# A mixture-of-experts stage in a one-core Trainium2 kernel: shift and scale of the routed rows moved from the experts' loop into the routing stage, onto GpSimd

## The chip, the cores and the metric

The kernel runs on one core of a Trainium2 chip. The metric is the device time of one execution in microseconds (us), as the median of several runs. The core has TensorE (PE, with its weight loads listed as PEld), VectorE (DVE), ScalarE (ACT), GpSimd (POOL) and SyncE (SP); SP computes nothing and issues most DMAs.

## The reference, cut to what matters

The reference is two transformer blocks in float32 (512 latent tokens and 256 context tokens of width 1024). The first block ends in a hierarchical mixture of experts, which is what the change is about:

```python
h = modulate(rms_norm(x, norm_ffn_g), shift, scale)      # h * (1 + scale) + shift
def hier_moe(h, w_rg, b_rg, w_re, b_re, w_gate, w_up, w_down):
    g_logits = hf @ w_rg + b_rg                          # 4 groups, the best one is taken
    e_logits = hf @ w_re + b_re                          # 32 experts, top 2 inside the group
    ...
    # rows of a token go to blocks of one expert, padded
    yb = (silu(xi @ w_gate[e]) * (xi @ w_up[e])) @ w_down[e]
    y = segment_sum(yb * row_w, row_tok)
```

`shift` and `scale` are two vectors of 1024 (one for all latent tokens), computed early from the conditioning vector; the gain `norm_ffn_g` is a third. The rms norm is a factor for each token; the modulation is a factor and a summand for each of the 1024 columns.

## The kernel before, in words

The program is one long sequence of stages. At the end of a stage every engine runs `fence` (line 222): it drains, counts up the semaphore `stage_done`, and the four compute engines wait for each other. SP isn't in the fence; its loads wait for semaphores and for given values of `stage_done`.

The last product ahead of the mixture (`pe_out`, `dve_resid`) ends at about 579 us; then fence 9 falls. In the **norm and routing stage** `act_norm` (line 447) sums squares, `dve_norm` (line 470) writes the four tiles of 128 tokens, scaled by their rms factor, to `XK(t)` (line 479), TensorE turns them (line 427), and ScalarE and VectorE shift and scale each turned quarter on its way out of PSUM into `hT` (lines 456 and 487), from which TensorE computes the router's logits (line 1557). SP stores `XK(t)`, only normed, to `xnd` in HBM as each tile is ready (line 3254). Then `dve_route` (line 1592) works out groups, experts, slots and weights in some seventy small operations on VectorE with a drain between most of them, with TensorE for prefix sums and for the list of token rows. The 128x1024 comparison `LOW` (line 1700) comes near its end. The last operation releases `rows_ok`; GpSimd, which has nothing else to do in this stage, waits for it and for the four stores, and gathers the first 128 rows from `xnd` (line 1725). Fence 10 falls.

Three small vectors, shift, scale and gain, come by three loads of 8 elements a partition at the start (`sp_route_params`, line 1541), and VectorE forms gain x (1 + scale) from them in column layout (line 1615).

The **experts' loop** (`sp_moe`, `pool_moe`, `pe_moe`, `act_moe`, `dve_moe`, lines 1741 to 1823) has 16 rounds here, each of two experts with 64 rows. Round i, in order: TensorE turns the 128x1024 gathered rows into PSUM banks 0 and 1 (line 1766). ScalarE takes bank 0 in four quarters and VectorE bank 1 in four quarters into `xgT`, and both shift and scale each quarter with one number a partition (lines 1797 and 1815). TensorE multiplies with the gate weights and the up weights (line 1775), ScalarE applies Silu (line 1801), VectorE multiplies (line 1820), TensorE turns the product (line 1780), ScalarE copies it out (line 1803), TensorE multiplies with the down weights (line 1788), VectorE applies the output gate vector (line 1823) and ScalarE's queue stores 128x1024 rows (line 1805). VectorE enters the loop only when the gate vector, loaded by ScalarE's queue after fence 10 (line 1396), is there. GpSimd gathers the next round's rows (line 1755) as soon as TensorE has turned the present ones. SP loads the six matrices of the next round (2 MB each, line 1739), the two of each kind as soon as their buffer has been used. The matrices of the first round are loaded during the stages before: up and down from 552 us, gate after fence 9.

Of the kernel before, what the change touches and what calls it, by code (L numbers as in the profile page):

```python
# [23 lines left out]
ALU = mybir.AluOpType  # L24
ACT = mybir.ActivationFunctionType
# [84 lines left out]
def program(nc, I, out):  # L110
    ctx = ExitStack()
    with ctx:
# [11 lines left out]
        def sem(name):  # L124
            return ctx.enter_context(nc.semaphore(name))
# [23 lines left out]
        def bank(b, n=BANK):  # L149
            return ps[:, b * BANK:b * BANK + n]  # L150
# [52 lines left out]
        v2a, a2v, v2p, prm = sem("v2a"), sem("a2v"), sem("v2p"), sem("prm")  # L203
        out_in, gate_in = sem("out_in"), sem("gate_in")
        rparams, zero_ok, rows_ok = sem("rparams"), sem("zero_ok"), sem("rows_ok")
        xg_in, xn_st = sem("xg_in"), sem("xn_st")
        w_used = [sem(f"w_used{m}") for m in range(3)]
        w_in_ = [sem(f"w_in{m}") for m in range(6)]
# [13 lines left out]
        def fence(eng, n):  # L222

            eng.drain().then_inc(stage_done, 1)  # L224
            n["fence"] += 4
            eng.wait_ge(stage_done, n["fence"])
# [319 lines left out]
        def plan_lin1(n):  # L546
            return Plan(n, "av" * 16 + "av")
# [131 lines left out]
        def plan_norm1(n):  # L679
            return Plan(n, "-" * (2 * TA))  # L680
# [717 lines left out]
        def plan_turn3(n, nt):  # L1398
            p = Plan(n, "v" * (2 * nt))
            p.g0 = n.get("t3", 0)  # L1400
            n["t3"] = p.g0 + 2 * nt
            return p
# [125 lines left out]
        EID = Z[0:1, 7780:7828].bitcast(I32)  # L1528
        NIT = Z[0:1, 7828:7829].bitcast(I32)
        SLOT, HS, LO8 = Z[:, 7640:7648], Z[:, 7648:7656], Z[:, 7656:7664]  # L1530
        TKB, IOTA, S8 = Z[:, 8800:8928], Z[:, 9824:9952], Z[:, 7664:7672]
        GE = Z[:, 5600:5800].rearrange("p (a j) -> p a j", j=25)
        HIT = Z[:, 5984:6176].rearrange("p (a j) -> p a j", j=24)
        LOW = Z[:, 8800:9824].rearrange("p (a j) -> p a j", j=P)
# [1 line left out]
        def sp_route_params(sp):  # L1536
            sp.dma_start(rw[:, :, 0:NG], I["router_group_w"][0].rearrange("(k p) n -> p k n", p=P)).then_inc(rparams, 16)
            sp.dma_start(rw[:, :, NG:NG + NE], I["router_expert_w"][0].rearrange("(k p) n -> p k n", p=P)).then_inc(rparams, 16)
            sp.dma_start(rb[:, 0:NG], I["router_group_b"][0].partition_broadcast(P)).then_inc(rparams, 16)
            sp.dma_start(rb[:, NG:NG + NE], I["router_expert_b"][0].partition_broadcast(P)).then_inc(rparams, 16)  # L1540
            for dst, src in ((fsh, modd[0, 0, 3 * D:4 * D]), (fsc, modd[0, 0, 4 * D:5 * D]), (fga, I["norm_ffn_g"][0])):
                sp.dma_start(dst, src.rearrange("(p k) -> p k", k=KT)).then_inc(rparams, 16)

        fsh, fsc, fga, fA = (small[:, 1240 + 8 * i:1248 + 8 * i] for i in range(4))

        def plan_route(n):
            return Plan(n, "vvvvv")
# [1 line left out]
        def pe_logits(pe):  # L1549

            def each(p, t):
                if t == 0:
                    pe.wait_ge(rparams, 16 * 7)
                for i in (2 * t, 2 * t + 1):
                    pe.wait_ge(EV[p.own[i]], p.val[i])
                for k in range(KT):
                    last = nc.tensor.matmul(bank(4)[:, 36 * t:36 * t + 36], hTk[:, k, 128 * t:128 * t + 128], rw[:, k, :],
                                            start=(k == 0), stop=(k == KT - 1))
                if t == TL - 1:
                    last.then_inc(mm_done, 1)  # L1560
            return each
# [30 lines left out]
        def dve_route(dve, n):  # L1592
# [18 lines left out]
                D_()  # L1611

            V.tensor_copy(TKB, C(C_TK, 1).broadcast_to([P, P])).then_inc(v2p, 1)
            dve.wait_ge(rparams, 16 * 7)
            V.scalar_tensor_tensor(fA, fsc, 1.0, fga, ALU.add, ALU.mult)
            dve.wait_ge(mm_done, p.done(0))
            V.tensor_tensor(LG, bank(4)[:, 0:36 * TL].rearrange("p (t n) -> p t n", t=TL), rb.unsqueeze(1).broadcast_to([P, TL, 36]),
                            ALU.add).then_inc(evac_v, 1)
# [77 lines left out]
            for c in range(2):  # L1696
                h = HIT[:, TL * c:TL * c + TL, :]
                V.tensor_tensor(h, h, C(C_TK, TL).unsqueeze(2).broadcast_to([P, TL, 24]), ALU.mult)
            D_()
            V.tensor_tensor(LOW, wide(LO8, P), IOTA.unsqueeze(1).broadcast_to([P, 2 * TL, P]), ALU.is_equal).then_inc(v2p, 1)  # L1700
            for c in range(2):
                V.tensor_copy(IDX[:, c, :], sc(10 + c))
# [18 lines left out]
        def pool_route(pool):  # L1721

            pool.wait_ge(rows_ok, 1)
            pool.wait_ge(xn_st, 16 * TL)
            pool.indirect_dma_start(xg, None, xnd, bass.IndirectOffsetOnAxis(ap=ROWS[:, 0:1].bitcast(U32), axis=0)).then_inc(xg_in, 16)
# [66 lines left out]
        def act_moe(act):  # L1792
            nit = trips(act)
            with act.Fori(0, nit) as i:
                act.wait_ge(xt_done, 2 * i + 3)
                for k in range(4):
                    last = act.activation(xgT[:, k, :], bank(0)[:, 128 * k:128 * k + 128], ACT.Identity,  # L1797
                                          scale=fA[:, k:k + 1], bias=fsh[:, k:k + 1])
                last.then_inc(xt_a, 1)
                act.wait_ge(w_used[0], i + 2)  # L1800
                act.activation(hg, bank(2), ACT.Silu).then_inc(silu_ok, 1)
                act.wait_ge(ht_done, i + 1)
                act.activation(hd, bank(4), ACT.Copy).then_inc(ht_a, 1)
                act.wait_ge(y_v, i + 1)
                act.dma_start(ybuf[bass.ds(i * P, P), :], yo).then_inc(y_out, 16)
            act.wait_ge(y_out, 16 * nit + 16)
            act.sem_inc(y_stored, 1)

        def dve_moe(dve, n):
            n["gate"] += 32  # L1810
            dve.wait_ge(gate_in, n["gate"])
            with dve.Fori(0, trips(dve)) as i:
                dve.wait_ge(xt_done, 2 * i + 4)
                for k in range(4):
                    last = nc.vector.tensor_scalar(xgT[:, 4 + k, :], bank(1)[:, 128 * k:128 * k + 128], fA[:, 4 + k:5 + k],
                                                   fsh[:, 4 + k:5 + k], ALU.mult, ALU.add)
                last.then_inc(xt_v, 1)
                dve.wait_ge(silu_ok, i + 1)
                dve.wait_ge(w_used[1], i + 2)
                nc.vector.tensor_tensor(hu, hg, bank(3), ALU.mult).then_inc(hu_ok, 1)  # L1820
                dve.wait_ge(w_used[2], i + 2)
                dve.wait_ge(y_out, 16 * i + 16)
                nc.vector.tensor_tensor(yo, ps[:, 5 * BANK:7 * BANK], gtb[:, 0, :], ALU.mult).then_inc(y_v, 1)
# [1406 lines left out]
        @block.sync  # L3230
        def _(sp):
            n, rel = tally(), [0, 0]
            sp_first(sp)
            plan_norm1(n)
            sp_lin1(sp, n, rel)
            sp.wait_ge(stage_done, 4 * 3)
            sp.dma_start(xl[:, 0:TL, :], I["x"][0].rearrange("(t p) d -> p t d", p=P)).then_inc(x_again, 16)
            for plan in (plan_gate, plan_dec, plan_st, plan_o):
                plan(n)
            plan_turn3(n, TL)  # L3240
            sp_out(sp, n, rel, I["w_out"][0], WO1, 0)
            sp.wait_ge(stage_done, 4 * 8)
            sp_route_params(sp)
            sp.dma_start(xl[:, TL:TA, :], I["ctx_2"][0].rearrange("(t p) d -> p t d", p=P)).then_inc(x_in, 16)
            for m in (1, 2):
                for x in range(2):
                    load_expert(sp, m, x, slice(x, x + 1))
            sp.wait_ge(stage_done, 4 * 9)
            for x in range(2):
                load_expert(sp, 0, x, slice(x, x + 1))  # L3250

            for t in range(TL):
                sp.wait_ge(xn_ok, TA + t + 1)
                sp.dma_start(xnd[P * t:P * t + P, :], XK(t)).then_inc(xn_st, 16)
            plan_norm(n, TL)
            plan_route(n)
            sp.wait_ge(stage_done, 4 * 10)
            sp_moe(sp)
            n["fence"] = 4 * 12
            plan_attn(n, *da_spec())  # L3260
            sp.wait_ge(stage_done, 4 * 12)
            for l in range(2):
                sp_layer(sp, n, rel, l)
            for t in LAT:
                sp.wait_ge(fin_ok, t + 1)
                sp.dma_start(out[0, P * t:P * t + P, :], yacc[:, t, :]).then_inc(out_in, 16)
            sp.wait_ge(stage_done, 4 * NF)
            sp.wait_ge(out_in, 64)

        @block.gpsimd  # L3270
        def _(pool):
# [23 lines left out]
            pool_glao(pool)  # L3295
            for _ in range(3):
                fence(pool, n)
            pool_route(pool)
            fence(pool, n)
            pool.dma_start(fng, I["final_norm_g"].partition_broadcast(P)).then_inc(fng_in, 16)  # L3300
# [1 line left out]
            fence(pool, n)  # L3302
            pool_comb(pool)
            fence(pool, n)
            plan_norm1(n)
            plan_lin1(n)
            for plan in (plan_gate, plan_dec, plan_st, plan_o):
                plan(n)
            plan_turn3(n, TL)
            plan_lin(n, WO1)  # L3310
            plan_norm(n, TL)
            plan_route(n)
            plan_attn(n, *da_spec())
            for l in range(2):
# [138 lines left out]
```

## Time and profile before

| | us |
|---|---|
| median of 3 runs | 3842.81 (3840.83 to 3851.01) |
| the profiled execution | 3844.6, its span 3842.7 |
| PE busy | 3374.2 (88%) |
| DVE busy | 1623.2 (42%) |
| ACT busy | 1132.2 (29%) |
| POOL busy | 617.5 (16%) |
| norm and routing stage | 579 to 627 |
| experts' loop | 639 to 1137 |

The busy times are sums over the whole span, with stages of different limits; what a change in one stage is worth has to be read in that stage. Times in the rows below are microseconds from the start of the span. The difference between a profiled execution's time and its span lies outside the span.

### The profile page before, as it was taken

The numbers are of one execution on the slowest core, as the hardware profiler recorded it, in microseconds if no ns is written. First come the engines' busy times: TensorE is split into PE (matmuls) and PEld (weight loads), VectorE is DVE, ScalarE is ACT, GpSimd is POOL, SyncE is SP. The second block draws the span as 40 slices with busy tenths as digits, with TensorE's granted clock in tenths as the row PEclk, the third lists the DMA queues.
The fourth block names the chain that finished last, engine by engine and source line by source line (L and its number), as shares of the span: only waits on it lengthen the run. The fifth ranks groups of instructions, "written<-read, shape, count | busy, mean of one in ns | idle before, by whom it ended". The sixth has DMA issues, their size and how long they took to land. (4 is left out here: it accounts for less than half of the span.)

```text
span 3842.7 us, 41657 instructions
## 1 busy us (share of the span) xinstructions
PE 3374.2 (88%) x16325; PEld 2395.6 (62%) x16325; DVE 1623.2 (42%) x2697; ACT 1132.2 (29%) x1921; POOL 617.5 (16%) x452
## 2 busy tenths in 40 slices
PE   4999875887766989789999799999799899988999
PEld 2666663222225865447887688888685457867887
DVE  3335653000015635563433533334574564345445
ACT  3113522111113235443222321221234444323222
POOL 1000000000003334123220100000345123301000
PEclk8999887899987999999999899999899999999999
DMA  6884034999986210002112312112521003224232
GB/s 255 327 323 164 3 123 190 428 428 428 428 353 204 62 25 11 9 36 84 57 55 88 112 65 66 60 62 88 161 73 35 9 36 107 84 107 138 88 99 88
DMA packets 162107, 534.00 MB, mean 139 GB/s; under 512 B 11917, under 2 KB 67077, under 8 KB 138893
## 3 DMA queue, kind: packets, MB, share of 16 engines
q1 hardware_dynamic: 139196, 401.22, 28.0%
q0 software_dynamic: 16256, 92.05, 6.8%
q10 hardware_dynamic: 6480, 38.34, 2.5%
q8 instruction: 117, 1.92, 0.2%
q14 instruction: 58, 0.47, 0.0%
HBM read 488.82 MB, written 42.76 MB: 138 GB/s over the span
## 5 line engine op out<-in xcount | busy, mean ns | idle before, releaser
L2981 PE MATMUL ps<-hT_hi,w_hi 128*128 128x512 f32 (+1 forms) x768 | 275.7, 359 | 24.6 <-DVE w_lo L2022 24.6
L2981 PE MATMUL ps<-hT_hi,w_lo 128*128 128x512 f32 (+1 forms) x768 | 276.3, 360 | 0.0
L2981 PE MATMUL ps<-hT_lo,w_hi 128*128 128x512 f32 (+1 forms) x768 | 275.9, 359 | 0.0
L2987 PE MATMUL ps<-w_hi,h_hi 128*128 128x512 f32 x640 | 253.7, 396 | 0.0
L2987 PE MATMUL ps<-w_hi,h_lo 128*128 128x512 f32 x640 | 253.7, 396 | 0.0
L2987 PE MATMUL ps<-w_lo,h_hi 128*128 128x512 f32 x640 | 253.6, 396 | 0.0
L2026 PE MATMUL ps<-wp_hi,hT_hi 128*128 128x512 f32 (+2 forms) x608 | 222.2, 365 | 30.6 <-DVE wp_lo L2022 29.1
L2243 PE MATMUL ps<-Z 64*128 64x256 f32 (+3 forms) x576 | 200.2, 544 | 29.1 <-DVE small L2385 12.2
L2027 PE MATMUL ps<-wp_lo,hT_hi 128*128 128x512 f32 (+2 forms) x608 | 220.2, 362 | 0.0
L2028 PE MATMUL ps<-wp_hi,hm_lo 128*128 128x512 f32 (+2 forms) x608 | 220.2, 362 | 0.0
L3004 ACT ACTIVATE w_hi<-ring 128x2048 fp32r<-128x2048 f32 x62 | 118.3, 1908 | 326.8 <-PE ps L2987 326.8
L2683 POOL TENSOR_TENSOR mr_lo<-ring,wm_hi 128x2048 fp32r<-128x2048 f32 x34 | 160.4, 4722 | 302.8 <-ACT wm_hi L2675 302.4
L1775 PE MATMUL ps<-ring,Z 128*64 128x512 f32 x512 | 144.2, 727 | 64.0 <-ACT Z L1797 59.9
L2026 PE MATMUL ps<-wm_hi,hT_hi 128*128 128x512 f32 x480 | 191.0, 398 | 8.8 <-ACT hT_hi L2739 8.8
L2027 PE MATMUL ps<-mr_lo,hT_hi 128*128 128x512 f32 x480 | 191.6, 399 | 0.0
L2027 PE MATMUL ps<-w_lo,hT_hi 128*128 128x512 f32 x480 | 191.2, 398 | 0.0
L2028 PE MATMUL ps<-wm_hi,hm_lo 128*128 128x512 f32 x480 | 191.1, 398 | 0.0
L2981 PEld LDWEIGHTS ps<-hT_hi,w_hi 128*128 128x128 f32 x768 | 145.0, 189 | 48.8 <-issue 25.0
L3038 DVE TENSOR_TENSOR w_lo<-ring,w_hi 128x2048 fp32r<-128x2048 f32 x62 | 142.1, 2292 | 76.4 <-ACT w_hi L3004 76.4
L3061 DVE TENSOR_TENSOR pj<-pj,ps 128x512 f32<-128x512 f32 x140 | 95.6, 686 | 167.4 <-PE ps L2987 167.4
L2981 PEld LDWEIGHTS ps<-hT_lo,w_hi 128*128 128x128 f32 x768 | 145.2, 189 | 24.6
L2981 PEld LDWEIGHTS ps<-hT_hi,w_lo 128*128 128x128 f32 x768 | 145.8, 190 | 23.0
(474 smaller groups left out, 6687.3 us busy)
## 6 DMA issues: line engine op xcount, KB each, us to landing
pj<-in_expert_w_up_dram SPq DMA_DIRECT2D x32, 2048.0 KB, 23.7
pj<-in_expert_w_down_dram SPq DMA_DIRECT2D x32, 2048.0 KB, 19.7
ring<-in_expert_w_gate_dram SPq DMA_DIRECT2D x32, 2048.0 KB, 15.5
ring<-in_ffn_w_dram SPq DMA_DIRECT2D x64, 1024.0 KB, 5.2
ring<-in_w_in_dram SPq DMA_DIRECT2D x58, 1024.0 KB, 5.4
Z<-in_w_mod_dram POOLq DMA_DIRECT2D x24, 2048.0 KB, 8.1
Z<-in_w_ada_dram POOLq DMA_DIRECT2D x8, 2048.0 KB, 8.7
ring<-in_w_out_dram SPq DMA_DIRECT2D x12, 1024.0 KB, 10.3
```

The costliest lines, as they stand in the source:

```text
L1775: last = nc.tensor.matmul(bank(2 + m)[64 * x:64 * x + 64, :], xgT[:, k, 64 * x:64 * x + 64], mslot[2 * m + x][:, 512 * k:512 * k + 512], s ...
L2026: nc.tensor.matmul(out_, a_hi, b_hi, start=first, stop=False)
L2027: nc.tensor.matmul(out_, a_hi, b_lo, start=False, stop=False)
L2028: return nc.tensor.matmul(out_, a_lo, b_hi, start=False, stop=final)
L2243: return nc.tensor.matmul(A.lat(u, x) if k0 == 0 else A.ctx(u, x), S["kq"](p, x, "q")[rs, P * t:P * t + P], S["kq"](p, x, "k")[rs, P * k0: ...
L2683: pool.tensor_tensor(mr_lo[:, 2048 * (x % 4):2048 * (x % 4) + 2048], mring[x % 4], wm_hi[:, 2048 * (x % 3):2048 * (x % 3) + 2048], ALU.sub ...
L2981: last = nc.tensor.matmul(bank(i % 8, c1 - c0), W[a][:, k, :], r[:, k, c0:c1], start=(k == 0 and r is hhk and a == 0), stop=(k == KT - 1 a ...
L2987: last = nc.tensor.matmul(bank(i % 8), H1[hb % 2][a][:, k, P * what:P * what + P], W[b][:, k, :], start=(k == 0 and a == b), stop=(k == 3 ...
L3004: act.activation(WHI[x % 2], raw[x % 4], ACT.Copy).then_inc(w_hi_ok, 1)
L3038: nc.vector.tensor_tensor(WLO[x % 2], raw[x % 4], WHI[x % 2], ALU.subtract).then_inc(w_lo_ok, 1)
L3061: nc.vector.tensor_tensor(y, y, bank(i % 8), ALU.add).then_inc(out_read, 1)
```

## The change

The rows that are stored to `xnd` are now normed, scaled and shifted, so that in the loop both engines only copy the turned rows. SP loads the three vectors as full rows, the same on all 128 partitions (512 KB each), after fence 9 and ahead of the gate weights. GpSimd forms (1 + scale) x gain, and then for each tile, once TensorE has turned it, multiplies and adds in place. SP stores a tile when GpSimd's sum for it is done. `RG` shares its place with `LOW`, so VectorE waits for GpSimd's first product before `LOW`.

```diff
+        mrow_in, mrow_ok, xm_ok = sem("mod_rows_in"), sem("mod_rows_ok"), sem("xm_ok")
...
-        TKB, IOTA, S8 = Z[:, 8800:8928], Z[:, 9824:9952], Z[:, 7664:7672]
+        RSH, RSC, RG = pj[:, 17408:18432], pj[:, 16384:17408], Z[:, 8800:9824]
+        TKB, IOTA, S8 = Z[:, 9952:10080], Z[:, 9824:9952], Z[:, 7664:7672]
...
-            for dst, src in ((fsh, modd[0, 0, 3 * D:4 * D]), (fsc, modd[0, 0, 4 * D:5 * D]), (fga, I["norm_ffn_g"][0])):
-                sp.dma_start(dst, src.rearrange("(p k) -> p k", k=KT)).then_inc(rparams, 16)
-
-        fsh, fsc, fga, fA = (small[:, 1240 + 8 * i:1248 + 8 * i] for i in range(4))
+
+        def sp_mod_rows(sp):
+            for dst, src in ((RSC, modd[0, 0, 4 * D:5 * D]), (RG, I["norm_ffn_g"][0]), (RSH, modd[0, 0, 3 * D:4 * D])):
+                sp.dma_start(dst, src.partition_broadcast(P)).then_inc(mrow_in, 16)
+
+        def pool_mod_rows(pool, p):
+
+            pool.wait_ge(mrow_in, 16 * 3)
+            pool.tensor_scalar(RSC, RSC, 1.0, 1.0, ALU.add, ALU.mult)
+            pool.drain()
+            pool.tensor_tensor(RSC, RSC, RG, ALU.mult)
+            pool.drain().then_inc(mrow_ok, 1)
+            for t in range(TL):
+                pool.wait_ge(mm_done, p.done(2 * t + 1))
+                pool.tensor_tensor(XK(t), XK(t), RSC, ALU.mult)
+                pool.drain()
+                pool.tensor_tensor(XK(t), XK(t), RSH, ALU.add).then_inc(xm_ok, 1)
...
-                    pe.wait_ge(rparams, 16 * 7)
+                    pe.wait_ge(rparams, 16 * 4)
...
-            dve.wait_ge(rparams, 16 * 7)
-            V.scalar_tensor_tensor(fA, fsc, 1.0, fga, ALU.add, ALU.mult)
+            dve.wait_ge(rparams, 16 * 4)
...
             D_()
+            dve.wait_ge(mrow_ok, 1)
             V.tensor_tensor(LOW, wide(LO8, P), IOTA.unsqueeze(1).broadcast_to([P, 2 * TL, P]), ALU.is_equal).then_inc(v2p, 1)
...
-                for k in range(4):
-                    last = act.activation(xgT[:, k, :], bank(0)[:, 128 * k:128 * k + 128], ACT.Identity,
-                                          scale=fA[:, k:k + 1], bias=fsh[:, k:k + 1])
-                last.then_inc(xt_a, 1)
+                act.activation(xgT[:, 0:4, :], bank(0).rearrange("p (k n) -> p k n", k=4), ACT.Copy).then_inc(xt_a, 1)
...
-                for k in range(4):
-                    last = nc.vector.tensor_scalar(xgT[:, 4 + k, :], bank(1)[:, 128 * k:128 * k + 128], fA[:, 4 + k:5 + k],
-                                                   fsh[:, 4 + k:5 + k], ALU.mult, ALU.add)
-                last.then_inc(xt_v, 1)
+                nc.vector.tensor_copy(xgT[:, 4:8, :], bank(1).rearrange("p (k n) -> p k n", k=4)).then_inc(xt_v, 1)
...
             sp.wait_ge(stage_done, 4 * 9)
+            sp_mod_rows(sp)
             for x in range(2):
                 load_expert(sp, 0, x, slice(x, x + 1))
 
             for t in range(TL):
-                sp.wait_ge(xn_ok, TA + t + 1)
+                sp.wait_ge(xm_ok, t + 1)
                 sp.dma_start(xnd[P * t:P * t + P, :], XK(t)).then_inc(xn_st, 16)
...
+            pool_mod_rows(pool, plan_norm(n, TL))
             pool_route(pool)
```

(On GpSimd the counting calls `plan_norm1`, `plan_lin1` and so on, which issue no instruction, move ahead of this call, so that it knows the counts of `mm_done`.)

## Rows read from the trace of the kernel before

**Rows 1.** Windows: busy us (count) of each engine, PE clock, DMA share, GB/s.

```profile
600.00:610.00 10.00, 3.12 (x15) 3.13 (x15) 5.85 (x28) 0.42 (x2) 0.00 (x0) 0.50 0.00 1
...
700.00:760.00 60.00, 50.52 (x216) 17.44 (x216) 6.37 (x12) 9.08 (x15) 1.75 (x4) 0.90 1.01 428
```

**Rows 2.** Timeline of one round of the loop: start, us, engine, line, operation [idle before].

```profile
882.43 1.22 DVE L1823 TENSOR_TENSOR Z<-ps,Z 128x1024 f32<-128x1024 f32 x1 [9.20 <-PE ps L1788]
...
884.51 1.28 ACT L1797 ACT_TABLE_LOAD   x1 [9.85 <-DVE Z L1823]
...
885.81 1.51 ACT L1797 ACTIVATE Z<-ps,small 128x128 f32<-128x128 f32 x4
...
887.37 8.41 PE L1775 MATMUL ps<-ring,Z 128*64 128x512 f32 x32 [3.98 <-ACT Z L1797]
...
897.27 7.09 PE L1775 MATMUL ps<-pj,Z 128*64 128x512 f32 x32 [1.49 <-DMA pj<-in_expert_w_up_dram]
...
905.92 0.60 ACT L1803 ACTIVATE Z<-ps 128x512 f32<-128x512 f32 x1 [9.49 <-PE ps L1780]
```

**Rows 3.** Groups of VectorE by form: busy us, mean ns, idle before.

```profile
L3059 DVE COPY pj<-ps 128x512 f32<-128x512 f32 x20 | 13.7, 690 | 26.5 <-PE ps L2987 26.5
```

**Rows 4.** Timeline at the start of the loop.

```profile
626.67 1.06 POOL L1725 DMA_INDIRECT Z<-xnd,Z  x1 [132.63 <-DVEq L224]
...
637.79 1.37 DVE L1815 TENSOR_SCALAR Z<-ps,small 128x128 f32<-128x128 f32 x4 [12.01 <-issue]
...
639.26 9.58 PE L1775 MATMUL ps<-ring,Z 128*64 128x512 f32 x32 [4.18 <-issue]
```

**Rows 5.** Timeline of the last round, and the window in which its weights end.

```profile
1111.98 8.75 PE L1775 MATMUL ps<-ring,Z 128*64 128x512 f32 x32 [3.98 <-ACT Z L1797]
...
1129.82 7.09 PE L1788 MATMUL ps<-pj,Z 128*64 128x512 f32 x32 [0.69 <-ACT Z L1803]
...
1127.00:1128.00 1.00, 0.59 (x4) 0.00 (x0) 0.35 (x1) 0.00 (x0) 0.00 (x0) 1.00 0.28 115
```

**Rows 6.** Timeline of the norm and routing stage.

```profile
579.42 0.80 SPq L1739 DMA_DIRECT2D ring<-in_expert_w_gate_dram  x2
...
589.47 0.74 DVE L479 TENSOR_SCALAR Z<-xl,small 128x1024 f32<-128x1024 f32 x1
...
601.38 0.49 DVE L1635 TENSOR_TENSOR Z<-Z 128x32 f32<-128x32 f32 x4
```

**Rows 7.** The same timeline: the gate vector's loads, 512 KB each.

```profile
631.55 0.81 ACTq L1396 DMA_DIRECT2D Z<-modd  x2
```

**Rows 8.** Groups of GpSimd by form: busy us, mean ns, idle before.

```profile
L2895 POOL TENSOR_SCALAR pj<-xl,small 128x1024 f32<-128x1024 f32 x11 | 16.0, 1471 | 227.0 <-DVE small L2864 227.0
...
L1307 POOL TENSOR_TENSOR pj<-pj,Z 128x512 f32<-128x512 f32 x4 | 4.9, 1264 | 157.1 <-DVEq L224 157.1
```

**Rows 9.** Timelines of VectorE and GpSimd in later stages where both run.

```profile
1237.47 4.47 DVE L1040 TENSOR_TENSOR Z<-pj 128x512 f32<-128x512 f32 x1
1242.01 0.69 DVE L1042 TENSOR_REDUCE small<-Z 128x8 f32<-128x512 f32 x1
1242.62 1.50 DVE L1040 TENSOR_TENSOR Z<-pj 128x512 f32<-128x512 f32 x1
...
1236.77 4.62 POOL L1985 TENSOR_TENSOR wp_lo<-ring,wp_hi 128x2048 fp32r<-128x2048 f32 x1 [3.24 <-ACT wp_hi L1971]
1241.35 2.22 POOL L1914 TENSOR_TENSOR Z<-Z,consts 128x896 f32<-128x896 f32 x1
...
2853.12 3.96 DVE L1044 TENSOR_SCALAR small<-small 128x4 f32<-128x4 f32 x1
...
2863.42 4.62 DVE L1040 TENSOR_TENSOR Z<-pj 128x128 f32<-128x128 f32 x1
...
2852.22 4.83 POOL L1985 TENSOR_TENSOR wp_lo<-ring,wp_hi 128x2048 fp32r<-128x2048 f32 x1 [11.39 <-ACT wp_hi L1971]
2863.26 4.63 POOL L1985 TENSOR_TENSOR wp_lo<-ring,wp_hi 128x2048 fp32r<-128x2048 f32 x1 [6.21 <-ACT wp_hi L1971]
```

More of the change, by code:

```diff
@@ L3297, in _ @@
                 fence(pool, n)
+            plan_norm1(n)
+            plan_lin1(n)
+            for plan in (plan_gate, plan_dec, plan_st, plan_o):
+                plan(n)
+            plan_turn3(n, TL)
+            plan_lin(n, WO1)
+            pool_mod_rows(pool, plan_norm(n, TL))
             pool_route(pool)
@@ L3304, in _ @@
             fence(pool, n)
[L3305 to L3311, printed above, removed]
             plan_route(n)
```

## The prediction

> **What bounds the kernel now.** The change touches two neighbouring stages, so I first read the windows by stage. They show two different limits. In the routing stage (about 597 to 627 us) VectorE works through a serial chain of small operations; between 600 and 610 us it is busy 5.85 of 10 us, GpSimd is busy 0, and the DMA engines are empty. In the experts' loop (639 to 1137 us, 16 rounds of 31.8 us) the DMA share is 1.01 at 428 GB/s in each of six windows of 60 us from 700 to 1060, of which the first is shown [rows 1]. A round moves six matrices of 2048 KB, one gather of 512 KB and one store of 512 KB, 13.6 MB: at 428 GB/s that is 31.8 us, exactly the round. The loop is bound by the weights' transfer.
>
> Next I read the timeline of one round [rows 2]. After the down product the queue in front of the gate product is: VectorE's scaling of the result (ends at 883.65), then on ScalarE (whose queue issues the store first) a table load of 1.28 us, four activations of 1.50 us together, then TensorE's gate product at 887.37. So ScalarE's turn costs 2.9 us that TensorE waits for. But the up product then waits 1.49 us for its own weights: what TensorE gains ahead of the gate product it returns there.
>
> **What goes in the loop.** ScalarE's four activations become one Copy of 128x512; the row for the same form (hd from a PSUM bank) is 0.60 us and is preceded by no table load [rows 2]. Gain in front of the gate product: 1.28 + 1.51 - 0.60 = 2.2 us a round. VectorE's four operations of 1.37 us together become one copy of 128x512 from PSUM, 0.69 [rows 3]: 0.7 us. If the Silu still gets a table load in each round, it lies under the gate product of over 8 us and costs nothing.
> - In rounds 1 to 14 I count nothing: the stream of weights covers it. Without that cover it would be 15 x 2.2 = 33 us.
> - In the first round the gate product waits for VectorE, which waits for the gate vector until 637.79 and ends at 639.16; TensorE starts at 639.26 [rows 4]. With one copy it starts 0.7 us sooner, and so does the first weight load of the loop and with it the whole stream: -0.7.
> - In the last round the stream has ended by 1127.3 [rows 5], while the down product starts only at 1129.82 and waits for ScalarE and so for the chain gate product, up product, turn. The gate product of that round starts at 1111.98; 2.2 sooner moves the down product to 1127.6, still just behind the last weights. So -2.2.
>
> About ScalarE's table: the rows show a load in front of the first Identity in each of the rounds, and none in front of the Copy. The Trainium skill, "ScalarE: Activation LUTs", section "Table sets: the hidden batching unit", says that cheap functions, copy and identity among them, are in every set. By that rule the load ahead of Identity would not be there and the exchange would give only 0.9 in place of 2.2; this trace does not bear it out.
>
> **What comes into the routing stage.** SP issues three row loads of 512 KB (128 x 4 KB) right after stage 9 closes at 579.42, in front of the two gate loads [rows 6]. The DMA engines are then idle. The nearest row is the gate vector: two such loads issued at 631.55 let VectorE go at 637.79, 6.2 us, with a third one beside them [rows 4, 7]. I take 7 us for three: 586.5. Ends: 585 (two loads' 6 us less the third beside them) and 590 (the 4 MB of gate weights behind them take part of the engines). The gate weights themselves land some 4 us later and are first used at 639: nothing. SP's three small loads that go away free its queue 2.5 us sooner for weights that nobody waits for: nothing. VectorE loses one small operation, 0.2.
>
> GpSimd then does one tensor-scalar of 128x1024, 1.5 us [rows 8], one product, and per tile a product and a sum: nine tensor-tensor of 128x1024. No row has that form. The row of 512 elements gives 1.26 us (2.47 ns an element), that of 2048 gives 4.62 (2.26) [rows 8, 9]; bounds 2.1 and 2.5, I take 2.3, nearest to the line between them, and 0.25 for the drain and the hand-over. 586.5 + 1.6 + 9 x 2.55 = 611 us is its end. The last tile's store is issued then and, at no more than the 6.2 us of the gate vector, is there by 617. The gather waits for the slots (626.67 before [rows 4]), so the stores are covered by 9 us and more. The new wait of VectorE ahead of the 128x1024 comparison (behind it are the last routing product and the gather) is fulfilled near 591, 29 us ahead: nothing.
>
> **What it does to VectorE** is the term that decides. The timelines of both engines show it against GpSimd's tensor-tensor [rows 9]: a 128x512 tensor-tensor of 0.68 lasts 4.47 us, until GpSimd's of 4.62 us has ended; the tensor-reduce behind it passes in 0.69; the next tensor-tensor takes 1.50, again until GpSimd's second has ended; and that second one took 2.22. Small ones are not spared: 128x128 lasts 4.62, a tensor-scalar of 128x4 3.96. So while GpSimd runs one tensor-tensor after another, VectorE gets about one operation that reads two SBUF tensors, or one in its fast form, through for each of them; reduces and operations on PSUM pass.
>
> Stepping VectorE's order through nine slots of 2.55 us from 588.1: the scalings of tiles 2 and 3 (589.47 before) take slots 1 and 2, the copy of the token column slot 4, the 16-element comparisons, product and subtraction of the first choice slots 5 to 8, the tensor-scalar after the exponential slot 9. At 611.3 VectorE stands where it stood at 601.38 [rows 6]. Each slot passes one operation which takes 0.3 us otherwise, so how many there are hardly matters: the delay is GpSimd's end less 601.3, and is **10 us**. Bounds: 585 with 2.1 a product gives 606.5 and 5 us; 590 with 2.5 gives 617 and 16 us; 0 if nothing is held. All behind it (slots, gather, fence, the gate vector's load, the first round) moves along, since nothing there waits for anything else: the engines are idle or in this chain.
>
> **The sum.** +10 - 0.7 - 2.2 = +7.1 us on the profiled execution's 3844.6 (span 3842.7, rest outside it unchanged): 3851.7. The median of the three runs lies 1.8 below that execution, so 3850. A measurement of this kernel can tell about 0.3%, 11.5 us, from no change.
>
> **The rivals.**
> - *VectorE is not held* (20%): the small operations slip in between GpSimd's, or GpSimd waits instead. For: no row has a chain of drained small operations. Against: [rows 9]. Then only the gain stays, -2.9: 3840; with a part of the holds up to 3845. The Trainium skill, "SBUF — State Buffer", section "Who interferes with whom", says that the loser blocks fully for the whole instruction; by that this rival would fall.
> - *The rows come late, GpSimd is slow* (16%), the other side: the three row loads share the engines with the gate weights and land at 590 or later, and each product is 2.5 plus 0.35 of waiting for VectorE's operation in between. GpSimd ends at 590 + 1.6 + 9 x 2.85 = 617.3, the delay is 16, the sum +13: 3856. It decides from a delay of 14.4 us on, which is a GpSimd end behind 615.7.
> - *The loop is not bound by its transfer* (3%): 2.2 us in each round, 33 us, less the delay of 10: 3820. Against it: DMA share 1.01, and 13.6 MB at 428 GB/s is the round.
> - *The exchange saves nothing in the loop* (the table load stays ahead of the Copy; 6%): then +10 - 0.7 - 0.9 = +8.4, 3851, hardly to be told apart from the forecast.
>
> **How the numbers follow.** The forecast has 55%. Same (within 0.3%) holds the forecast, the first and the last rival: 0.80; slower 0.17, faster 0.03. The range reaches from the first rival with its 1 us less, 3839, to the late case, 3858.
>
> **What would show it.** Right: VectorE's small operations in the routing stage with durations near 2 us, one for each GpSimd product; the first gather issued near 636 instead of 626.67; rounds still 31.8 us, with the gate product starting 2.2 us sooner behind the down product and the up product waiting 3 to 4 us for its weights. Wrong: the gather at 627 (nothing held), or behind 641 (the late case, or the stores ending the wait); rounds of under 31.5 us; a table load still in front of ScalarE's Copy.

## The result, and the profile after

The kernel after takes 3854.14 us, the kernel before 3846.76 (medians of 20 runs each); the ratio is 1.002 with a 95% interval of 1.0014 to 1.0026. The change costs 7.4 us by the medians, where +7.1 was forecast. (The 3842.81 of the table above is the median of the first three of the runs before.) The profiled execution of after took 3849.9 us, its span 3848.0, 5.3 over the span before.

Two executions differ by some microseconds in stages that no line of the change touches, so I count from points inside the trace: from the first sum of squares behind fence 9 (579.42 before, 577.30 after) to VectorE's last operation of the routing stage, to the issue of the first gather, and from there to the last result's scaling behind the loop.

| us | before | after |
|---|---|---|
| fence 9 to VectorE's last operation | 46.18 | 54.80 |
| fence 9 to the first gather | 47.25 | 55.31 |
| first gather to the last result's scaling | 510.38 | 508.15 |

The span's +5.3 is then: -2.1 ahead of fence 9 (another execution), +8.1 in the routing stage, -2.2 in the loop, +1.6 behind it (again another execution; nothing there was changed).

The timeline of VectorE after, from the end of the norms into the first choice; it answers to [rows 6]:

```profile
587.35 1.24 DVE L480 TENSOR_SCALAR Z<-xl,small 128x1024 f32<-128x1024 f32 x1
588.51 1.36 DVE L488 TENSOR_SCALAR hT<-ps,small 128x128 f32<-128x128 f32 x4
589.79 1.56 DVE L480 TENSOR_SCALAR Z<-xl,small 128x1024 f32<-128x1024 f32 x1
...
594.37 1.59 DVE L1629 COPY Z<-consts 128x128 f32<-128x128 f32 x1
...
597.49 0.91 DVE L1620 TENSOR_TENSOR Z<-Z 128x16 f32<-128x16 f32 x1
598.48 2.22 DVE L1622 TENSOR_TENSOR Z<-Z,consts 128x16 f32<-128x16 f32 x1
600.77 0.17 DVE L1624 TENSOR_REDUCE Z<-Z 128x4 f32<-128x16 f32 x1
601.01 2.17 DVE L1626 TENSOR_TENSOR Z<-Z 128x16 f32<-128x16 f32 x1
603.25 2.22 DVE L1640 TENSOR_TENSOR Z<-Z 128x16 f32<-128x16 f32 x1
...
606.10 1.86 DVE L1646 TENSOR_SCALAR Z<-Z 128x16 f32<-128x16 f32 x1
607.87 0.48 DVE L1650 TENSOR_TENSOR Z<-Z 128x32 f32<-128x32 f32 x4
```

And that of GpSimd in the same stretch, with the gather behind it:

```profile
584.49 1.04 POOL L1551 TENSOR_SCALAR pj<-pj 128x1024 f32<-128x1024 f32 x1 [91.66 <-DMA pj<-modd]
585.69 2.36 POOL L1553 TENSOR_TENSOR pj<-pj,Z 128x1024 f32<-128x1024 f32 x1 [0.15 <-issue]
588.22 2.59 POOL L1557 TENSOR_TENSOR Z<-Z,pj 128x1024 f32<-128x1024 f32 x1 [0.18 <-issue]
...
603.11 2.34 POOL L1557 TENSOR_TENSOR Z<-Z,pj 128x1024 f32<-128x1024 f32 x1
605.59 2.34 POOL L1559 TENSOR_TENSOR Z<-Z,pj 128x1024 f32<-128x1024 f32 x1
632.61 1.08 POOL L1741 DMA_INDIRECT Z<-xnd,Z  x1 [24.69 <-DVEq L1735]
```

The two are to be read side by side. Operations on 16 elements last 2.2 us: the one that starts at 598.48 ends at 600.7, where GpSimd's instruction of 598.33 (2.34 us) ends; the tensor-reduce behind it takes 0.17 and isn't held; the next one lasts until 603.18, again to the end of GpSimd's next instruction. The four quarters from PSUM (588.51) keep their 1.36. From 607.93, when GpSimd is done, every duration is as before. Line 1650 is line 1635 of before: it stood at 601.38 - 579.42 = 21.96 us behind the fence, and now at 30.57.

The loop. The timeline of one round after answers to [rows 2]:

```profile
889.75 0.34 ACTq L1818 DMA_DIRECT2D ybuf<-Z  x1
890.44 1.28 ACT L1812 ACT_TABLE_LOAD   x1 [9.37 <-DVE Z L1833]
...
891.74 0.60 ACT L1812 ACTIVATE Z<-ps 128x512 f32<-128x512 f32 x1
892.35 1.28 ACT L1814 ACT_TABLE_LOAD   x1
892.39 7.09 PE L1791 MATMUL ps<-ring,Z 128*64 128x512 f32 x32 [3.08 <-ACT Z L1812]
...
901.97 7.09 PE L1791 MATMUL ps<-pj,Z 128*64 128x512 f32 x32 [2.49 <-DMA pj<-in_expert_w_up_dram]
```

The Copy takes 0.60 in place of 1.51 us, but the table load in front of it stays: TensorE waits 3.08 us ahead of the gate product where it waited 3.98. The windows and the waits of the loop after:

```profile
700.00:760.00 60.00, 45.47 (x211) 17.52 (x212) 3.43 (x5) 8.33 (x10) 1.79 (x3) 1.00 1.01 428
...
1000.00:1060.00 60.00, 48.64 (x206) 17.94 (x202) 5.02 (x6) 8.71 (x10) 2.30 (x4) 0.91 1.01 428
...
PE ps L1791 <- ACT Z L1812: 46.2, 15, 3.1
PE ps L1791 <- DMA pj<-in_expert_w_up_dram: 31.9, 13, 3.7
```

In the waits of before the same two were:

```profile
PE ps L1775 <- ACT Z L1797: 59.9, 15, 4.0
...
PE ps L1775 <- DMA pj<-in_expert_w_up_dram: 8.0, 7, 1.5
```

TensorE waits 13.7 us less for ScalarE and 23.9 us more for the up weights, at the same 428 GB/s as in [rows 1]. The second figure is larger because several gate products are shorter too (7.09 us at 892.39 in place of 8.4 to 9.5 us before), and it scatters: in e1, e2, e3, e8 and e10 below, which have the same loop, TensorE waits 9.5 to 33.1 us for the up weights beside the same 46 us for ScalarE. The 15 rounds between the first and the last gate product take 472.7 us before and 471.0 after.

### The profile page after: what moved, and what is told of

The parts are those of the page before. It is cut to its first block and busy times, and to the rows that moved or that the text cites. A ratio compares the mean times of both kernels' runs of the same rounds, so it can differ in the third digit from the quotient of the medians.

```text
span 3848.0 us, 41576 instructions
## 1 busy us (share of the span) xinstructions
PE 3362.2 (87%) x16325; PEld 2392.5 (62%) x16325; DVE 1623.4 (42%) x2648; ACT 1117.7 (29%) x1873; POOL 641.5 (17%) x462
## 5 line engine op out<-in xcount | busy, mean ns | idle before, releaser
L2253 PE MATMUL ps<-Z 64*128 64x256 f32 (+3 forms) x576 | 201.6, 544 | 28.7 <-DVE small L2395 12.6
L1791 PE MATMUL ps<-ring,Z 128*64 128x512 f32 x512 | 125.5, 647 | 49.9 <-ACT Z L1812 46.2
```

Source lines behind the costliest of these rows:

```text
L1791: last = nc.tensor.matmul(bank(2 + m)[64 * x:64 * x + 64, :], xgT[:, k, 64 * x:64 * x + 64], mslot[2 * m + x][:, 512 * k:512 * k + 512], s ...
L2253: return nc.tensor.matmul(A.lat(u, x) if k0 == 0 else A.ctx(u, x), S["kq"](p, x, "q")[rs, P * t:P * t + P], S["kq"](p, x, "k")[rs, P * k0: ...
```

## The experiments

Theory: GpSimd's nine reading instructions hold VectorE in the routing stage, and the transfer of the weights hides what the loop gains. Rivals: the late stores, the row loads or the denser stage cost the time; the loop's exchange has another value than it seems. The last columns of this table are read as above; ratios are to the kernel before.

| kernel | fence 9 to VectorE's last operation | first gather to last scaling | ratio, 95% |
|---|---|---|---|
| before | 46.18 | 510.38 | |
| after | 54.80 | 508.15 | 1.002 (1.0014 to 1.0026) |
| e1, GpSimd only writes | 46.39 | 509.62 | 0.9995 (0.9986 to 1.0004) |
| e2, products alone | 46.89 | 509.25 | 0.9994 (0.9984 to 1.0003) |
| e3, before with copying loop | 46.19 | 509.36 | 0.9996 (0.9987 to 1.0005) |
| e4, after with old loop | 54.84 | 509.37 | 1.002 (1.001 to 1.0029) |
| e8, turned back, late | 50.37 | 508.98 | 1.0007 (0.9998 to 1.0017) |
| e9, the same, turned loop | 50.35 | 510.47 | 1.0015 (1.0006 to 1.0024) |
| e10, turned back, in order | 46.27 | 510.93 | 0.9996 (0.9988 to 1.0005) |
| e11, the same, turned loop | 46.26 | 510.29 | 1.0006 (0.9997 to 1.0015) |

**e1: GpSimd as busy, but only writing.**

```diff
+            def busy():
+                for _ in range(2):
+                    last = pool.memset(pj[:, 16384:17604], 0.0)
+                    pool.drain()
+                return last
...
-            pool.tensor_tensor(RSC, RSC, RG, ALU.mult)
+            busy()
...
-                pool.tensor_tensor(XK(t), XK(t), RSC, ALU.mult)
-                pool.drain()
-                pool.tensor_tensor(XK(t), XK(t), RSH, ALU.add).then_inc(xm_ok, 1)
+                busy()
+                busy().then_inc(xm_ok, 1)
```

> The kernel after, but each of GpSimd's nine products and sums of the routing stage is replaced by two memsets of 1220 columns into the place of the row vectors, so GpSimd is busy for about as long (2.3 us each time) and only writes. Shift and scale of the experts' rows are left out. Routing time is counted from the first sum of squares after fence 9 to the issue of the first gather: 47.3 us before, 55.3 after. Theory (VectorE's operations that read two SBUF tensors, and its fast forms, are held while GpSimd's instruction reads): routing time falls to 47 to 48.5 us, the comparisons of the first choice take 0.17 to 0.3 us again, total near the kernel before, ratio 0.999 to 1.000. Rival (the late stores, the row loads or GpSimd's occupation itself delay the stage): it stays at 55 us, the stores being as late as after.

From GpSimd's and VectorE's timeline of this kernel:

```profile
590.88 20.29 POOL L1553 MEMSET pj<- 128x1220 f32 x16 [0.22 <-issue]
...
592.40 1.64 DVE L480 TENSOR_SCALAR Z<-xl,small 128x1024 f32<-128x1024 f32 x1
...
597.00 0.65 DVE L1633 COPY Z<-consts 128x128 f32<-128x128 f32 x1
...
600.13 0.18 DVE L1624 TENSOR_TENSOR Z<-Z 128x16 f32<-128x16 f32 x1
600.38 0.17 DVE L1626 TENSOR_TENSOR Z<-Z,consts 128x16 f32<-128x16 f32 x1
...
601.92 0.63 DVE L1650 TENSOR_SCALAR Z<-Z 128x16 f32<-128x16 f32 x1
```

GpSimd is busy to 611.2, 31.2 us behind the fence, as long as after, and the stores are as late. Yet VectorE's last operation comes at 46.39 us; the tensor-tensor operations that lasted 0.91 and 2.22 us take 0.18 and 0.17. All but 0.2 us of the delay of 8.6 us is gone, though row loads, late stores and the new wait are all still there. Some operations that read one SBUF tensor are still held beside the memsets: the scalings of tiles 2 and 3 take 1.23 and 1.64 us, as long as after, the copy of the token column 0.65 us in place of 0.21, and the tensor-scalar behind the exponential 0.63 in place of 0.14. The two-input operations of the chain are held only beside the reading instructions. Whether a GpSimd instruction that reads one tensor instead of two would hold them as well was not tested.

**e2: five reading instructions in place of nine.** The line with `ALU.add` is left out and its signal stands at the product.

> The kernel after without the four sums (the shift of the experts' rows is left out): five tensor-tensor on GpSimd in place of nine. Theory (one held operation for each GpSimd instruction, so the delay is GpSimd's end less the point VectorE had reached): GpSimd ends about 20.6 us behind fence 9, when the first choice's chain has hardly begun; routing time 48 to 49.5 us, a delay of 1 to 2. Rival (VectorE slowed in proportion to GpSimd's work): delay 5/9 of 8.1, so 51.7 us.

The timelines of GpSimd and VectorE of this kernel:

```profile
586.27 9.97 POOL L1557 TENSOR_TENSOR Z<-Z,pj 128x1024 f32<-128x1024 f32 x4 [0.18 <-issue]
...
595.51 0.75 DVE L1618 TENSOR_TENSOR Z<-Z 128x16 f32<-128x16 f32 x1
596.34 0.18 DVE L1620 TENSOR_TENSOR Z<-Z,consts 128x16 f32<-128x16 f32 x1
```

The delay is 0.7 us, not 5/9 of 8.6. GpSimd ends at 596.24, inside the first comparison of the choice; before that point VectorE reads mostly PSUM and few of its operations are held. So the four sums, with which GpSimd ends 9.7 us later behind the fence (30.6 in place of 20.9), cost 7.9 us of VectorE's time, and five products alone cost 0.7. (From the fence to the gather it was 47.41, under the 48 to 49.5 expected: the gather follows VectorE's last operation by 0.52 us in place of 1.07, see the last section, and the delay itself was under the 1 to 2 expected.)

**e3 and e4: the two halves of the change apart.** e3 is the kernel before with the loop of after:

```diff
-                for k in range(4):
-                    last = act.activation(xgT[:, k, :], bank(0)[:, 128 * k:128 * k + 128], ACT.Identity,
-                                          scale=fA[:, k:k + 1], bias=fsh[:, k:k + 1])
-                last.then_inc(xt_a, 1)
+                act.activation(xgT[:, 0:4, :], bank(0).rearrange("p (k n) -> p k n", k=4), ACT.Copy).then_inc(xt_a, 1)
```

and VectorE's alike; e4 is the kernel after with the reverse edit and the three column vectors loaded and formed as before.

> The kernel before with nothing changed but the loop: ScalarE and VectorE only copy the turned rows, so shift and scale of the experts' rows are left out. Theory (the loop is bound by the weights' transfer): routing time 47.3 us as before; from the first gather to the last result's scaling 508.2 us in place of 510.4, as in the kernel after; ratio 0.9994, not to be told from 1. Rival (the exchange pays in each round, 0.9 us by the rows of after): 496 us, ratio 0.996.

> The kernel after with the loop of before (four operations a bank with the column vectors, loaded and formed again), so shift and scale are applied twice. Theory: routing time 55.3 us as after, loop 510.4 us as before; total 2.2 us over the kernel after, ratio to before 1.002 to 1.003. If the loop's part of the change were larger than it seems, the loop would take over 512 us here.

e3 has the routing time of before, e4 that of after; the loss lies wholly in the routing stage. The loop shows no such order: 509.36 us with copies in e3, where 508.2 was expected, 509.37 with four operations in e4, where 510.4 was expected, and over all copying loops 508.2 to 510.9. What the exchange gives there is under this scatter of 2.8 us from profile to profile. The 2.2 us less in the one profile of after can't be put down to the exchange.

**e5, e6, e7: the loop without its cover.** In the rounds SP loads half of each matrix:

```diff
-                        load_expert(sp, m, x, bass.ds(e[x], 1))
+                        sp.dma_start(mslot[2 * m + x][:, 0:HALF // 2], WE[m][bass.ds(e[x], 1)].rearrange("a (p k) n -> p (a k n)", p=P)[:, 0:HALF // 2]).then_inc(w_in_[2 * m + x], 16)
```

e5 has the old loop, e6 the copying one, and e7 turns ScalarE's loop:

```diff
+            take(3)
+            with act.Fori(1, nit) as i:
+                act.wait_ge(w_used[0], i + 1)
+                act.activation(hg, bank(2), ACT.Silu).then_inc(silu_ok, 1)
+                act.wait_ge(ht_done, i)
+                act.activation(hd, bank(4), ACT.Copy).then_inc(ht_a, 1)
+                act.wait_ge(y_v, i)
+                act.dma_start(ybuf[bass.ds(i * P - P, P), :], yo).then_inc(y_out, 16)
+                take(2 * i + 3)
...
```

(`take` waits for the turned rows and issues the Copy; the last round's part stands behind the loop.)

> The kernel before, but in the loop SP loads only half of each expert's matrix (1 MB in place of 2 MB; the experts' weights are wrong from the second round on). A round then moves 7.3 MB, 17 us at 428 GB/s, so TensorE's chain must be the bound. Summed from the rows of the kernel after, with no wait for weights: 27.7 us a round with copies and 0.9 more with four operations a bank, so 28.6 us here. This one alone tells nothing between the theories; it is the base for the next.

> The same with the copying loop (shift and scale left out). Theory (the exchange is worth 0.9 us a round, which the transfer of the weights hides in the full kernel): 27.7 us a round, 0.9 less than with half loads and the old loop. Rival (the exchange is worth nothing on TensorE's chain in any case, since another wait takes its place): the same round.

> The same again, with ScalarE's loop turned: the first Copy stands ahead of the loop and each round begins with the Silu and ends with the next round's Copy. Theory (the table load in front of the Copy is there because the Copy is the first activation behind the loop's head): the load ahead of the Copy is gone, one load a round or none, at the Silu, hidden; 26.4 us a round, 1.3 less. Rival (each Copy behind a Silu costs a load): two loads a round still, 27.7 us.

TensorE's gate products in a round of e5, e6 and e7:

```profile
883.36 9.46 PE L1775 MATMUL ps<-ring,Z 128*64 128x512 f32 x32 [3.99 <-ACT Z L1797]
```

```profile
902.31 8.78 PE L1775 MATMUL ps<-ring,Z 128*64 128x512 f32 x32 [3.08 <-ACT Z L1796]
```

```profile
897.81 7.09 PE L1775 MATMUL ps<-ring,Z 128*64 128x512 f32 x32 [1.58 <-ACT Z L1797]
```

The rounds are 30.72, 29.01 (28.88 and 29.14 in turn) and 25.93 us, where 28.6, 27.7 and 26.4 were expected; the times of the one run of each are 3836.83, 3808.16 and 3764.12 us. So the exchange does pay where the weights come fast enough: 1.7 us a round, and turning the loop 3.1 more. Both are larger than the ScalarE time they save (0.9 and 1.5), since the gate product gets shorter as well, from 9.46 us to 8.53 and 8.79 in turn and then to 7.09. What makes it shorter is TensorE's granted clock. In e5 it falls to its lower level (0.50, which is 1.2 GHz) while TensorE idles ahead of the gate product, and stays there through its first half. From the windows of e5:

```profile
883.00:884.00 1.00, 0.64 (x2) 0.29 (x4) 0.00 (x0) 0.98 (x2) 0.00 (x0) 0.50 0.96 352
...
887.00:888.00 1.00, 1.00 (x6) 0.30 (x4) 0.00 (x0) 0.00 (x0) 0.00 (x0) 0.50 1.00 410
...
889.00:890.00 1.00, 1.00 (x6) 0.28 (x4) 0.00 (x0) 0.00 (x0) 0.00 (x0) 1.00 0.00 0
```

In e7 it is at its upper level (2.4 GHz) in every window around the gate product of 897.81, one of which is:

```profile
899.00:900.00 1.00, 1.00 (x6) 0.29 (x4) 0.00 (x0) 0.06 (x1) 0.00 (x0) 1.00 0.95 369
```

The length of the wait ahead of it doesn't settle the gate product's time by itself: behind the same 3.08 us it takes 8.53 or 8.79 us in e6, 7.09 or 8.78 after, and up to 10.07 in e3.

e7 also settles the table load. The groups of ScalarE between 640 and 1030 us:

```profile
L1802 ACT ACT_TABLE_LOAD x14 | 18.0, 1283 | 0.3
L1797 ACT ACTIVATE Z<-ps 128x512 f32<-128x512 f32 x15 | 9.0, 597 | 137.3 <-DVE Z L1828 137.3
```

One load a round is left, at the Silu (line 1802), which now stands at the loop's head; the Copy (line 1797) has none. Before and after, each round has two, one at the head (Identity or Copy) and one at the Silu (892.35 above). The head's load belongs to the first activation behind the head of the loop, whichever it is, not to the function.

**e8 to e11: the same result without GpSimd.** `hT` holds the shifted and scaled rows, turned, for the logits. TensorE turns its 32 blocks back, ScalarE copies them to the rows' place, SP stores them; the row loads and GpSimd's work go.

```diff
+            for i in range(2 * TL):
+                if i >= 4:
+                    pe.wait_ge(xm_ok, i - 3)
+                for k in range(4):
+                    last = nc.tensor.transpose(bank(i % 4)[:, P * k:P * k + P],
+                                               hTk[:, 4 * (i % 2) + k, P * (i // 2):P * (i // 2) + P], ident)
+                last.then_inc(back_done, 1)
...
                 act.activation(dst, src, ACT.Exp).then_inc(a2v, 1)
+                if first_exp:
+                    first_exp = False
+                    for i in range(2 * TL):
+                        act.wait_ge(back_done, i + 1)
+                        act.activation(XK(i // 2)[:, 512 * (i % 2):512 * (i % 2) + 512], bank(i % 4), ACT.Copy).then_inc(xm_ok, 1)
```

In e8 and e9 the condition was `n["v2a"] % 2`, by which the copies stood behind the second exponential instead of the first. e9 and e11 have ScalarE's turned loop besides.

> All of the computation, with the copying loop of after, but the shifted and scaled rows come from hT, which holds them turned for the logits: TensorE turns its 32 blocks back (about 5 to 7 us between the logits and the prefix sums, where it idles 8), ScalarE copies eight banks to the rows' place (4.8 us between its two exponentials, where it idles 6), SP stores each tile. GpSimd does nothing in this stage and the row loads are gone. Theory (only GpSimd's reading instructions cost the 8 us): routing time 46.9 to 48 us, the comparisons of 0.2 to 0.3 us, total as the kernel before or 1 to 2 us under it, ratio 0.9985 to 1.0. Rival (the late stores or the denser stage cost by themselves): 50 us and more.

> The kernel that turns hT back, with ScalarE's turned loop. Theory (bound by transfer): the gate product starts 1.3 us sooner behind the down product in each round, the up product waits as much longer, and the loop is at most 1.3 us shorter, 507 to 509 us from the gather; ratio to before 0.999 to 1.0. Rival: 1.3 us in each of 15 rounds, 20 us, ratio 0.994.

> The kernel that turns hT back, mended in its order: ScalarE copies the eight banks right behind its first exponential (before, they stood behind the second, so TensorE's second half of the turning back stood in the way of the prefix sums: last operation of VectorE 50.4 us behind fence 9 in place of 46.2). Theory (the 4.2 us came from that order, the late stores cost nothing): 46.2 to 47 us, the loop as in the copying kernels (509.3 from the gather), total 1 us under the kernel before, ratio 0.999 to 1.0005. Rival (TensorE's turning back costs the routing chain in any order): over 48.5 us.

> The same with ScalarE's turned loop. Theory (transfer binds the loop): rounds of 31.8 us on average once the lead is used up, though half loads let the same chain run in 25.9; from the gather to the last result 507.5 to 509.5 us; ratio to before 0.998 to 1.0005. Rival (the faster chain pays in the full kernel too): under 500 us.

TensorE's timeline in e8 and then in e10, with ScalarE's copies of e10 in the fence behind it:

```profile
593.86 1.91 PE L1569 MATMUL ps<-consts,hT 128*128 128x128 f32 x16
602.82 3.68 PE L1569 MATMUL ps<-consts,hT 128*128 128x128 f32 x16 [7.04 <-ACT Z L1598]
606.28 4.32 PE L1577 MATMUL ps<-Z,consts 128*128 128x32 f32 x20
```

```profile
594.74 1.91 PE L1569 MATMUL ps<-consts,hT 128*128 128x128 f32 x16
597.51 2.12 PE L1569 MATMUL ps<-consts,hT 128*128 128x128 f32 x16 [0.86 <-ACT Z L1600]
602.89 4.48 PE L1577 MATMUL ps<-Z,consts 128*128 128x32 f32 x20 [3.27 <-DVE Z L1653]
```

```profile
596.87 4.00 ACT L1600 ACTIVATE Z<-ps 128x512 f32<-128x512 f32 x8
602.94 0.20 ACT L1595 ACTIVATE Z<-Z 128x4 f32<-128x4 f32 x1 [2.07 <-DVE Z L1654]
```

In e8 the second half of the turning back stood in front of the prefix sums and cost 4.2 us. My expectation missed that: the first gather came 51.5 us behind the fence, on the rival's side (50 and more), and only e10 tells this order apart from a cost of the late stores. In e10 it fits: 4.0 us of TensorE and 4.0 us of ScalarE in a gap that VectorE's chain leaves them, and VectorE is done at 46.27 us, 0.1 over before. e10 does all of the computation, and is at 0.9996 (0.9988 to 1.0005) of before against 1.002 for after: the rows modulated ahead of the loop for nothing, and nothing won either, since the loop is covered. e11 shows the cover most plainly. With half loads the same loop runs in 25.9 us a round (e7); here it needs 510.3 us from the gather, as before, and TensorE waits 53.2 us for the up weights:

```profile
PE ps L1784 <- DMA pj<-in_expert_w_up_dram: 53.2, 14, 4.6
...
PE ps L1784 <- ACT Z L1806: 23.6, 15, 1.6
```

No version among these is measurably faster than the kernel before. The two with the turned loop missed their expectations: e9 came out at 1.0015 where at most 1.0 was expected, e11 at 1.0006 where at most 1.0005 was, and their loops at 510.5 and 510.3 us lie over the 509 and 509.5 expected. Their ratios are 0.0008 above e8's and 0.001 above e10's; the intervals overlap, so a cost of the turned loop isn't shown, nor is it ruled out.

## Why the prediction was right

**The row loads.** Forecast: there 7 us behind the first issue, from the gate vector's 6.2. Measured: issued at 577.29, GpSimd starts at 584.49, 7.2.

**GpSimd's price.** Forecast 1.5 us for the tensor-scalar and 2.55 for each of nine slots, the end 31.6 us behind the fence. Measured 1.04, and 2.49 from start to start, the end at 30.6. The form that no row had takes 2.34 us, inside the bounds of 2.1 and 2.5 and next to the 2.3 taken.

**The hold.** The slots came as stepped through: the scalings of tiles 2 and 3 at 1.24 and 1.56 us in place of 0.74, the copy of the token column, then four small operations of the first choice and the tensor-scalar behind the exponential. The rule "GpSimd's end less the place where VectorE had stood" gives 30.6 - 22.0 = 8.6 us; measured 8.62. The 10 us of the forecast were 1.4 too long: 1.0 is GpSimd's end (30.6 behind the fence in place of 31.6), the rest the slots counted to 611.3 and the rounding. (GpSimd's instructions beside VectorE's scalings took 2.59 and 2.62 us in place of 2.34, so GpSimd was held a little as well.) e1 shows that the cause is GpSimd's reading and not its being busy, the loads or the stores, and e2 that only instructions which meet VectorE's chain count. The first rival (not held) falls with the durations of up to 2.22 us; the second (rows late, GpSimd slow) had the right mechanism and the wrong sizes.

**The covers.** The last store was issued at 608, the gather at 632.6: 24 us. The wait ahead of the 128x1024 comparison was fulfilled at 588.1, 39 us early.

**The loop: the step that failed.** Forecast: the Copy is preceded by no table load, so 2.2 us a round go, and the last round gives 2.2. That came from a Copy in the middle of a round, the line for `hd`, and its neighbourhood is what mattered: the load belongs to the loop's head (e7). It stayed, and the exchange was worth 0.9 us to ScalarE, the fourth rival, to which I gave 6%. With it falls what I wrote of the Trainium skill's rule in "ScalarE: Activation LUTs", section "Table sets: the hidden batching unit", that copy and identity are in every set. The trace doesn't speak against it: after, the Identity of line 457 (585.21) follows a Sqrt (582.69) and has no load ahead of it, and in e7 the Copy has none behind the Silu. I had laid to the function what belongs to the place.

The total came out closer than its terms, and that is luck. Up to the first gather the change cost 8.1 us in place of 10: the hold was 8.6, and the gather then followed 0.5 us sooner, which no term had. The loop gave back 0.7 us by the medians (7.4 less 8.1) in place of 2.9. The two errors, of about 2 us each, cancel; and by the interval of the ratio the change costs 5.4 to 10.0 us, so 7.4 beside 7.1 is closer than the measurement is sure. Of the loop's terms only the first round's can be seen: the first gate product starts 12.1 us behind the gather in place of 12.6 (0.5 of the forecast 0.7). The last round's, 0.9 by ScalarE's rows in place of 2.2, is under the scatter that e3 and e4 show. The third rival (the exchange pays in each round) falls with e3 and e11.

**"Bound by the transfer" was true of the whole and not of each round.** The gate products of before start 30.7 to 30.9 us apart in the first six rounds, as in e5 with half of the loads, and no up product waits for its weights there: TensorE's chain sets the round, out of weights whose loads run ahead. Only from the seventh (823.83) to the last (1111.98) do they average 32.0, and three rounds in turn take 95.5, 31.8 each, from 855.53 to 951.06. A DMA share of 1.01 says that the queue always had work, not that someone waited for it.

## What to carry to other kernels

A stage of many small VectorE operations in series is the wrong place for GpSimd instructions that read SBUF, however idle GpSimd is there: one VectorE operation that reads two SBUF tensors gets through for each of them, so the price here was about GpSimd's whole time past the start of the chain. Writing instructions, or TensorE and ScalarE in gaps that the chain leaves them, cost 0.1 to 0.2 us (e1, e10). And before work is taken out of a loop, ask what its round waits for: here the exchange was worth 1.7 us a round with half of the weights' loads and nothing that could be measured with all of them.

## What the runs showed of the hardware that I had not expected

- A tensor-tensor of VectorE on 16 elements a partition, 0.18 us alone, lasts up to 2.22 us beside a reading GpSimd instruction, and 0.17 to 0.18 beside memsets of the same total length (e1). A scaling of 128x1024, with one SBUF tensor as input, is held beside memsets too, 1.64 us in place of 0.74 (e1).
- The first gather follows VectorE's last operation by 1.07 us when GpSimd has been waiting for 131 us or more (before, e3, e8, e10), and by 0.51 to 0.52 when it has been waiting for 15 to 27 (after, e1, e2, e4). What the half microsecond is stays open.
- The table load of the activation at the head of this loop is issued in every round, 1.28 us each, and turning the loop so that another activation stands there moves it (e7).
- TensorE's gate product takes 7.09 us behind 1.58 us of idleness, at the upper clock, and 9.46 behind 3.99, half of it at the lower one, so that 0.9 us taken from ScalarE gave 1.7 us a round, and 1.5 us gave 3.1 (e5 to e7).
